# Two plain up pairs instead of three ahead of the halved products, in the first third of three FFNs

## What is computed

```
def swiglu(x, w1, w3, w2):
    return (jax.nn.silu(x @ w1) * (x @ w3)) @ w2

x = x + 0.5 * swiglu(rms_norm(x, ffn1_norm[l]), ffn1_w1[l], ffn1_w3[l], ffn1_w2[l])
...                                   # mixing
x = x + 0.5 * swiglu(rms_norm(x, ffn2_norm[l]), ffn2_w1[l], ffn2_w3[l], ffn2_w2[l])
```

## Time and profile before

| | |
|---|---|
| median of 3 runs | 2742.47 us (2742.37 to 2743.11) |
| profiled execution | 2742.97 us |
| its span | 2741.2 us |
| PE busy | 2735.9 us (100%) |
| VectorE (DVE) busy | 1927.5 us (70%) |
| ScalarE (ACT) busy | 1374.6 us (50%) |
| GpSimd (POOL) busy | 970.2 us (35%) |

### The profile page before, as it was taken

The page is one execution under the profiler, slowest core; times in us unless marked ns, Lnnn a source line. Parts: engine busy times, 40 slices in busy tenths (PEclk is TensorE's granted clock), DMA queues, the critical chain, the costliest instruction groups (busy, mean ns, idle before and its releaser), DMA issues.

```text
span 2741.2 us, 42858 instructions
## 1 busy us (share of the span) xinstructions
PE 2735.9 (100%) x16342; PEld 2344.8 (86%) x16342; DVE 1927.5 (70%) x3192; ACT 1374.6 (50%) x2215; POOL 970.2 (35%) x482
## 2 busy tenths in 40 slices
PE   9999999999999999999999999999999999999999
PEld 8898888777788889999998988887777888899998
DVE  7686857885667447888785778578856674588885
ACT  6353444655355446455563534446553653454553
POOL 0134824433343442232121357244333434432331
PEclk9999999999999999999999999999999999999999
DMA  5333583222222223233332335732222222323322
GB/s 171 108 107 117 150 181 109 78 76 70 85 85 85 85 93 101 93 116 105 108 108 93 116 115 156 175 108 78 77 70 80 90 81 89 97 93 104 108 102 100
DMA packets 113262, 285.19 MB, mean 104 GB/s; under 512 B 35632, under 2 KB 45360, under 8 KB 112560
## 3 DMA queue, kind: packets, MB, share of 16 engines
q1 hardware_dynamic: 113072, 282.61, 33.2%
HBM read 268.93 MB, written 9.44 MB: 102 GB/s over the span
## 4 chain that ended last, share of the span: by engine, by line
PE 99%; DVE 0%; DMA 0%; ACT 0%; issue 0%; SPq 0%; ACTq 0%; DVEq 0%
PE bank L653 21%; PE bank L654 21%; PE bank L655 21%; PE bank L702 8%; PE bank L703 8%; PE bank L704 8%; PE bank L679 1%; PE bank L680 1%; PE bank L681 1%; PE bank L1117 1%; PE bank L1136 1%; PE bank L1151 1%; PE bank L886 1%; PE bank L1250 1%; PE bank L1104 0%; PE bank L1309 0%
## 5 line engine op out<-in xcount | busy, mean ns | idle before, releaser
L495 POOL TENSOR_TENSOR w_lo<-raw,w_hi 128x1024 fp32r<-128x1024 f32 x208 | 519.9, 2503 | 872.1 <-ACT w_hi L487 872.1
L653 PE MATMUL bank<-h_hi,w_hi 128*128 128x512 f32 x1504 | 593.3, 395 | 0.5 <-DVE silu_a L2502 0.3
L655 PE MATMUL bank<-h_hi,w_lo 128*128 128x512 f32 x1504 | 585.9, 390 | 0.0
L654 PE MATMUL bank<-h_lo,w_hi 128*128 128x512 f32 x1504 | 585.8, 390 | 0.0
L567 POOL TENSOR_TENSOR w_lo<-raw,w_hi 128x1024 fp32r<-128x1024 f32 (+1 forms) x138 | 253.0, 1854 | 765.7 <-DVE bank L2423 695.3
L487 ACT ACTIVATE w_hi<-raw 128x1024 fp32r<-128x1024 f32 x294 | 309.3, 1056 | 287.6 <-PE bank L655 249.6
L653 PEld LDWEIGHTS bank<-h_hi,w_hi 128*128 128x128 f32 x1504 | 282.3, 188 | 65.7 <-issue 7.1
L655 PEld LDWEIGHTS bank<-h_hi,w_lo 128*128 128x128 f32 x1504 | 282.3, 188 | 59.9
L654 PEld LDWEIGHTS bank<-h_lo,w_hi 128*128 128x128 f32 x1504 | 282.5, 188 | 56.4
L1692 ACT ACTIVATE t_hi<-bank 128x512 fp32r<-128x512 f32 x276 | 162.6, 599 | 207.1 <-DVE bank L2421 61.7
L653 PE MATMUL bank<-g_hi,w_hi 128*128 128x512 f32 x570 | 222.1, 390 | 0.0
(11 more groups left out here) (494 smaller groups left out, 6226.0 us busy)
## 6 DMA issues: line engine op xcount, KB each, us to landing
raw<-in_w_lots SPq DMA_DIRECT2D x478, 512.0 KB, 3.6
s_wd<-s_z SPq DMA_DIRECT2D x8, 512.0 KB, 2.7
s_t<-s_taps SPq DMA_DIRECT2D x16, 256.0 KB, 11.0
da_s<-da_qk SPq DMA_DIRECT2D x16, 256.0 KB, 4.1
x<-in_x SPq DMA_DIRECT2D x8, 256.0 KB, 5.5
raw_k<-in_w_lots SPq DMA_DIRECT2D x8, 256.0 KB, 5.8
s_w_im<-s_wd SPq DMA_DIRECT2D x32, 64.0 KB, 4.2
s_w_re<-s_wd SPq DMA_DIRECT2D x32, 64.0 KB, 3.0
```

The costliest lines, as they stand in the source:

```text
L495: eng.tensor_tensor(w_lo[:, s], raw[:, s], w_hi[:, s].bitcast(f32), SUB).then_inc(S["lo_done"], 1)
L653: pe.matmul(b[:, :], w_hi[:, s, kw], xh[:, k], start=(k == 0), stop=False)
L654: pe.matmul(b[:, :], w_hi[:, s, kw], xl[:, k], start=False, stop=False)
L655: return pe.matmul(b[:, :], w_lo[:, s, kw], xh[:, k], start=False, stop=(k == nk - 1))
```

## The change

The number of plain pairs in the three places goes from 3 to 2; the third pair, lots n+4 and n+5, becomes a halved one. `three_plain` becomes `two_plain`. On ScalarE `high(n+5)` and `high(n+6)` go, the roundings of the weight sums (`round_weights`, now of n+4) move from behind the first `round_g` to a place between `rstd_of` and the first silu, and the third silu goes. On VectorE the low parts of lots n+4 and n+5 go (GpSimd now makes them), the sums T1 and T3 of lots n+4 and n+5 come directly behind the low parts of the sums of h, the rest of the sums comes behind pair 0's multiplications by `rstd` and ahead of its multiplication by silu. The engines' `halved` then begins at lot n+4.

```diff
-PLAIN_PAIRS = (((6, 0, 6), (3, 0, 6)), ((3, 0, 0), (3, 0, 0)))
+PLAIN_PAIRS = (((6, 0, 6), (2, 0, 6)), ((2, 0, 0), (2, 0, 0)))
...
# ScalarE
-            def three_plain(n, g, which):
+            def two_plain(n, g, which):
 
                 whole = 0 in DOWN_HALVED[which]
                 high_sum(2 * which)
                 round_s(which)
                 high(act, n + 4)
-                high(act, n + 5)
                 rstd_of(2 * which)
+                round_weights(n + 4)
                 silu(n, 0, g)
                 round_g(0, g, whole)
-                high(act, n + 6)
-                round_weights(n + 6)
                 silu(n + 2, 1, g)
-                round_g(1, g, whole)
-                silu(n + 4, 0, g)
...
# VectorE
-            def three_plain(n, g, which):
+            def two_plain(n, g, which):
 
                 whole = 0 in DOWN_HALVED[which]
                 low_sum(2 * which)
                 sums_of_h(which)
-                V.wait_ge(S["lo_done"], LOT(n + 4))
-                low_of(V, n + 4)
-                low_of(V, n + 5)
+                add_t(n + 4, T1)
+                add_t(n + 4, T3)
                 V.wait_ge(S["rstd_ready"], R(2 * which + 1))
                 pair_of_plain(n, 0)
+                low_t(n + 4, T1)
+                add_t(n + 4, T2)
+                low_t(n + 4, T3)
+                low_t(n + 4, T2)
+                add_t(n + 4, T4)
+                low_t(n + 4, T4)
                 multiply(0, g, whole)
                 if not whole:
                     low_g(0, g)
-                weights_t(n + 6)
                 pair_of_plain(n + 2, 1)
                 multiply(1, g, whole)
-                if not whole:
-                    low_g(1, g)
-                pair_of_plain(n + 4, 2)
-                multiply(2, g, whole)
```

More of the change, by code:

```diff
@@ L1841, in ffn1 @@
                         else:
-                            three_plain(n, g0, 0)
+                            two_plain(n, g0, 0)
                     if i0 < J:
@@ L1881, in ffn2 @@
                     if th == 0:
-                        three_plain(n, g0, 1)
+                        two_plain(n, g0, 1)
                     halved(n, i0, J, g0, th in DOWN_HALVED[1])
```

## The result

| | before | after |
|---|---|---|
| median | 2742.59 us (10 runs, 2742.2 to 2743.45) | 2749.74 us (10 runs, 2748.92 to 2751.51) |
| span of the profiled execution | 2741.2 us | 2747.8 us |
| ratio | | 1.0027, 95% interval [1.0019, 1.0035] |

The change makes the kernel slower by 7.1 us, 0.27%. The interval leaves out no change. The forecast was 2747.9, in a range of 2745.4 to 2750.6; the median is inside the range and 1.8 us above the forecast.

What follows compares the result with a forecast made beforehand. PE's back-to-back matmuls were taken as the bound: 2 x 2.55 (A, C) + 2.9 (B) of waits, less 2.57 saved, gave +5.4 us, so 2742.47 became 2747.9 us, range 2745.4 to 2750.6.

Steps and rivals of the forecast that it cites:

- B: Place: first third of layer 1's first FFN, which also makes low_g; forecast to lose 2.9 us before the matmul saving.
- q6 waits 2.25 at A and C: First halved pair: PE's product q6 waits 2.25 us for copy_x, ScalarE's copy of q1's bank; bounds none and 4.2.
- A: Place: first third of layer 0's second FFN; forecast to lose 2.55 us before the matmul saving.
- C: Place: first third of layer 1's second FFN; same code and spacing as A, forecast to lose 2.55 us before the matmul saving.
- The table load is on the path and hides no drain: ScalarE: silu's 1.28 us load, formerly hidden, follows T4's rounding ahead of copy_x; a drain, 1.4 us per place, had 2%.
- B: 2.15 and 0.8: Layer 1's first FFN: q6 waits 2.15 us for copy_x, then q7 0.8 us for VectorE's take_y (bounds 0 and 1.4).
- Lag of the second pair: A and C: VectorE's 0.5 us of lag costs the second halved pair's q7 0.15 us (between 0 and 0.5), nothing later.
- restarts: PE: each wait costs about 0.08 to 0.1 us on restart; two restarts at A and C, 0.15 us.
- Rival (3): VectorE doesn't regain its lag, so each later pair's q7 pays about 0.25 us; +3.0, 2750.9 us; chance 11%.
- GpSimd's takeover costs nothing: First halved pair at A: GpSimd makes the low parts in 3.66 us, ending near 54.3, before PE's 56.03.
- rival (4): TensorE's clock falls behind the waits, +4.3 to +8.6 us with one or two products each; 2752.2 or more; chance 5%.
- the forecast's own mechanism: PE waits at q6 for copy_x at all three places; 2747.2 to 2748.6 us; chance 75%.

Runs made afterwards that it cites:

- e1: Changed kernel plus a one-column silu on ScalarE directly behind rstd_of, so the function table loads early; 2744.40 us, ratio to before 1.0006.
- e3: Changed kernel with the early table load, high(n+6), copy_x, copy_v and take_y moved ahead, low_g(1) behind take_y; 2746.19 us, ratio to before 1.0012.
- e8: Changed kernel with early table load, high(n+6) behind silu(0), copy_x and copy_v behind silu(1), take_y ahead of low T1; 2741.66 us, ratio to before 0.9996.
- e5: Changed kernel with 18 extra matmuls between q5 and q6 of the first halved pair at all three places; 2748.25 us, ratio to before 1.002.
- e2: Changed kernel with high(n+6) and copy_x ahead of round_g(0) and silu(1) on ScalarE, table load still late; 2751.98 us, ratio to before 1.0035.
- e4: Kernel before the change, with two plain pairs only in layer 0's second FFN, three at the two other places; 2745.82 us, ratio 1.0011.
- e7: Changed kernel with only low_g(1) in layer 1's first FFN moved behind low T1 and take_y on VectorE; 2750.92 us, ratio to before 1.0028.
- e6: Changed kernel with eight chained one-column copies more on ScalarE behind silu(1), ahead of copy_x, at the three places; 2757.40 us, ratio to before 1.0052.

## Why the prediction was right

- *PE's list of matmuls is the bound, and the change can act only by 2.57 us less or by new waits*: right. The halved pairs keep their 10.03 (after, B's steady pairs start at 1418.52, 1428.52 and 1438.57), and outside the three places no stretch changed by more than 0.24 us.
- *q6 waits 2.25 at A and C*: 2.01 of idle time, and q6 started 2.16 later than it would have without a wait (1060.81 - 1058.65, where q5's matmuls end). VectorE's first silu multiplication, expected 57.88 - 49.31 = 8.57 behind the point where it came free, was at 1057.58 - 1049.07 = 8.51; `copy_x` ended at 1060.75, 4.95 behind q1's start, forecast 5.06. Each link of the chain from T4's rounding to `copy_x` was within 0.1 us, since each had a row. One bound doesn't add up: ten hand-offs at 0.2 in place of 0.04 give 2.25 + 1.6 = 3.85 us and not 4.2. Nothing rests on it.
- *The table load is on the path and hides no drain*: right; with the load out of the way in e1, each wait fell by 1.3 us, the load alone, with nothing for a drain.
- *B: 2.15 and 0.8*: 1.90 and 0.74 of idle time; B as a whole grew by 2.04, forecast 2.05.
- *Lag of the second pair, 0.15, and restarts, 0.15*: at A and B the second pair's q7 came some 0.2 us late, each restart cost 0.1 more, and the steady pairs lost nothing. Rival (3), a lag carried on, did not occur.
- *GpSimd's takeover costs nothing*: right; its w_lo of the new halved pair ran from 1050.50 for 3.66 us at A. But its work for the *second* halved pair has little slack: once PE no longer waited long at the first pair, this work held PE for 0.3 to 0.5 us (e3 at all places, e8 at B). The prediction didn't look there; in the changed kernel no wait for it shows, as PE came to the second pair later.
- *The sum*: forecast +5.4, measured +5.5 where TensorE isn't idle and its clock stays at 1.00 behind q6 (e5). The term that was mis-sized is the clock, which stood at zero in the forecast and as rival (4) with 5%: it does fall behind some of these waits. In the median it is worth 1.5 us, much less than rival (4)'s 4.3 to 8.6, as it falls in part of the places (and, by the spread of the times, of the executions) and for some 3 us only. Rival (4) also priced it too high: at 0.50 the matmuls of C start 0.21 us apart and not at twice the 0.12. With it the result is 1.0027, where the forecast stood on the edge at 1.002. So the mechanism was right, and that the median lies in the range is in part luck: it is above the 2747.2 to 2748.6 of the forecast's own mechanism, in a part of the range that was there for rival (3), which did not occur. The row that I had against rival (4), 1.06 us of idleness at the start, was half as long as the wait that I foresaw, and so was no evidence.

That the intended gain is there, and lost to the order of ScalarE's and VectorE's queues, is shown by e8's places, 1.04 us under before in sum in one trace; its times don't show it beyond their interval.

## What to carry to other kernels

When the bound engine is brought to a point earlier, list what the *other* engines have queued ahead of the first thing it needs there, and sum the chain from rows: a lead of one 10.88 us step was cut and paid for by a chain that had been hidden, in which a table load of 1.28 us was the longest single instruction. The function table can be loaded by a one-column activation at a point where the engine has time, as e1 did. Two gates that open at nearly the same time must be moved together (e2 moved one and lost 2.2 us more), and a moved operation is to be checked against what GpSimd does in its new place.

## What the runs showed that was not expected

- TensorE idle for 2.0 us in a full stream of matmuls sometimes loses its clock: in the changed kernel's profiled execution at C (PEclk 0.50 for some 3 us, 1.3 us lost) and not at A with the same 2.01 us. Over the traces of the change, e2, e4 and e7 there are nine waits of 1.9 to 2.0 us, and the clock fell behind three. What decides it is not shown. With idleness of 0.7 us at three places (e1) it never did in the trace; with 3.9 us (e6) it did at all three, for 1.0 to 2.1 us each. Such waits probably give the kernel its spread: 2.6 us between ten runs of the change, 1.3 in e5 and 0.7 in e8, over eleven runs each.
- A VectorE subtraction of two SBUF tiles took 2.17 and 1.09 us in place of 0.69 while GpSimd subtracted SBUF tiles, ending both times 0.5 us behind GpSimd's operation; those with an operand in PSUM kept their 0.69.
